# Two later layers' attention: maxima of the last two heads together, one bank for head outputs, another K tile order behind them

## The reference

```
for l in range(2):
    h = rmsnorm(x, norm_w[l])
    proj = h @ w_in[l]
    y_ssd = ssd_branch(...)          # 1024 features, ends in an rmsnorm over them
    y_cfm = conformer_branch(...)    # 512 features
    y_att = diff_attention_branch(...)  # 512 features, 4 heads of 128
    x = x + concat([y_ssd, y_cfm, y_att]) @ w_out[l]

diff_attention_branch, for each of 4 heads:
    s = q k^T / 8 for two halves c = 0, 1; causal mask; p = softmax(s)
    w = p[0] - lam * p[1];  o = w @ v
    o = rmsnorm(o, subln_w) * (1 - lambda_init);  result = o * silu(z)
```

## Time and profile before

| | us |
|---|---|
| median of three runs | 3719.62 (3715.02 to 3720.99) |
| the profiled execution | 3718.19 |
| its span in the trace | 3716.4 |
| TensorE busy | 3490.1, 94% of the span |
| VectorE busy | 1951.4, 53% |
| ScalarE busy | 545.5, 15% |

### The profile page before, as it was taken

The page is one execution under the profiler, slowest core; times in us unless marked ns, Lnnn a source line. Parts: engine busy times, 40 slices in busy tenths (PEclk is TensorE's granted clock), DMA queues, the critical chain, the costliest instruction groups (busy, mean ns, idle before and its releaser), DMA issues.

```text
span 3716.4 us, 54843 instructions
## 1 busy us (share of the span) xinstructions
PE 3490.1 (94%) x23714; PEld 2920.6 (79%) x23714; DVE 1951.4 (53%) x2736; ACT 545.5 (15%) x1020; POOL 161.1 (4%) x166
## 2 busy tenths in 40 slices
PE   6999999987889899998999999999899979999979
PEld 2445475545778889987999999998889958889958
DVE  2256942225667736533666667444375660375650
ACT  1000011223434321001100000000101120101120
POOL 0000001000000000000000000000040000140000
PEclk9999999998979999999999999999899989999979
DMA  8878633103322254443444444544344304344313
GB/s 344 329 308 323 260 110 114 57 3 92 81 70 70 59 202 170 170 170 125 159 165 169 163 169 169 183 180 159 109 152 149 136 35 147 114 152 155 125 38 133
DMA packets 134752, 559.44 MB, mean 151 GB/s; under 512 B 57504, under 2 KB 61856, under 8 KB 72112
## 3 DMA queue, kind: packets, MB, share of 16 engines
q1 hardware_dynamic: 120256, 456.17, 35.2%
q10 hardware_dynamic: 14304, 100.42, 6.8%
HBM read 539.24 MB, written 17.30 MB: 150 GB/s over the span
## 4 chain that ended last, share of the span: by engine, by line
PE 68%; DVE 4%; ACT 2%; issue 1%; SPq 1%; DMA 1%; DVEq 0%; ACTq 0%
PE ps L463 19%; PE ps L2576 13%; PE ps L2973 10%; PE ps L2632 7%; PE ps L2150 6%; PE ps L1590 2%; PE ps L3379 1%; PE ps L1688 1%; PE ps L1593 1%; DVE arena L2035 1%; DVE arena L2037 1%; SPq L1411 0%; PE ps L3085 0%; PE ps L3387 0%; PE ps L1569 0%
## 5 line engine op out<-in xcount | busy, mean ns | idle before, releaser
L463 PE MATMUL ps<-arena,ring 128*128 128x256 f32 (+3 forms) x4224 | 1073.3, 417 | 43.7 <-issue 20.2
L463 PEld LDWEIGHTS ps<-arena,ring 128*128 128x128 f32 (+1 forms) x4224 | 811.7, 193 | 304.2 <-issue 193.8
L2576 PE MATMUL ps<-arena 128*128 128x128 f32 x2560 | 292.4, 275 | 0.0
L2576 PEld LDWEIGHTS ps<-arena 128*128 128x128 f32 x2560 | 289.1, 192 | 0.0
L2576 PE MATMUL ps<-arena,ring 128*128 128x128 f32 x1920 | 220.9, 275 | 0.0
L2576 PEld LDWEIGHTS ps<-arena,ring 128*128 128x128 f32 x1920 | 217.7, 192 | 0.1
L2973 PE MATMUL ps<-arena 128*128 128x128 f32 x1792 | 204.7, 275 | 0.0
L2973 PEld LDWEIGHTS ps<-arena 128*128 128x128 f32 x1792 | 202.4, 192 | 0.0
L794 DVE SCALAR_TENSOR_TENSOR arena<-arena,small 128x512 f32<-128x512 f32 x240 | 180.4, 752 | 36.6 <-DMA arena<-in_ada_late 20.1
L2632 PE MATMUL ps<-arena 128*128 128x128 f32 x1408 | 161.2, 275 | 0.0
L2632 PEld LDWEIGHTS ps<-arena 128*128 128x128 f32 x1408 | 159.2, 192 | 0.0
(11 more groups left out here) (496 smaller groups left out, 4327.7 us busy)
## 6 DMA issues: line engine op xcount, KB each, us to landing
ring<-in_weights SPq DMA_DIRECT2D x402, 1024.0 KB, 4.8
arena<-in_ada_late ACTq DMA_DIRECT2D x64, 1024.0 KB, 8.0
arena<-in_gates SPq DMA_DIRECT2D x56, 256.0 KB, 3.7
arena<-in_front ACTq DMA_DIRECT2D x8, 1024.0 KB, 9.1
arena<-in_x ACTq DMA_DIRECT2D x2, 2048.0 KB, 12.5
keep_g<-arena SPq DMA_DIRECT2D x14, 256.0 KB, 2.0
arena<-keep_h SPq DMA_DIRECT2D x3, 1024.0 KB, 6.1
arena<-in_ctx ACTq DMA_DIRECT2D x1, 2048.0 KB, 23.6
```

The lines of the kernel that those rows point to most:

```text
L463: mm = M.matmul(o, ring[:, slot, k, c0:c0 + w], rhs, start=(kc == 0), stop=(kc == ktiles * WK - 1))
L2576: mm = M.matmul(o, w[:, k], x(k), start=(k == 0), stop=(k == HD - 1))
```

## The change

Three things are moved in both later layers; no arithmetic is added or taken away.
- The heads. PE's list has the same order. On ACT `turn(1)` now stands ahead of `exps(2)`, and `exps(3)` follows `exps(2)`. On DVE `outs(0)`, `outs(1)`, then `maxes` of heads 2 and 3, then `mix` of both, then the last two `outs`. All head outputs go through bank 7, so `values(h)` waits for `outs(h - 1)` from h = 1 on (before: from h = 2 on, for `outs(h - 2)`).
- The output product. `column_block` and `pairs` are replaced by `out_tiles`, which takes some K tiles of a block. The order is block 0 K tile 0, head norms, block 0 K tile 1, block 1 K tiles 0 and 1, block 0 K tiles 2 and 3, block 1 K tiles 2 and 3, then blocks 2 and 3 whole, without a loop. The wait for `om_in` stands ahead of block 1, the third wait for `y_part` ahead of block 0's K tile 2.
- The packed array has tiles 2 to 5 of `w_out_2` in the new order.

```diff
@@ packing
-        out += [...] + [_tiles(a['w_out_2'][l])]
+        out += [...] + [_tiles(a['w_out_2'][l])[OUT2_ORDER]]
+OUT2_ORDER = [0, 1, 4, 5, 2, 3, 6, 7, 8, 9, 10, 11, 12, 13, 14, 15]
@@ att_pe
-                if h >= 2:
+                if h >= 1:
                     p.wait_ge(at['o_in'].sem, at['o_in'].due(p))
-                o = ps[:, 6 + h % 2, 0:T]
+                o = ps[:, 7, 0:T]
...
+            def out_tiles(b, kts, first, last):
+                for kt in kts:
+                    slot = take_tile(p)
+                    for n in range(4):
+                        for k in range(WK):
+                            mm = M.matmul(ps[:, 4 * (b % 2) + n, 0:T], ring[:, slot, k, n * P:(n + 1) * P], yv[:, 4 * kt + k],
+                                          start=(kt == first and k == 0), stop=(kt == last and k == WK - 1))
+                            if n == 0 and k == 0:
+                                mm.then_inc(slot_left.sem, slot_left.up(p))
+                    if kt == last:
+                        mm.then_inc(bo.full[b % 2].sem, bo.full[b % 2].up(p))
...
-            column_block(p, bo, 0, 4, out_moving, before=(ssd_part, lambda: None, conformer_part, attention_part))
-            column_block(p, bo, 1, 4, out_moving)
-            pairs(p, 1, 4, out_moving, bo)
+            p.wait_ge(bo.free[0].sem, bo.free[0].due(p))
+            p.wait_ge(y_part.sem, y_part.due(p, 2))
+            out_tiles(0, (0,), 0, 3)
+            head_norms()
+            out_tiles(0, (1,), 0, 3)
+            p.wait_ge(bo.free[1].sem, bo.free[1].due(p))
+            p.wait_ge(at['om_in'].sem, at['om_in'].due(p))
+            out_tiles(1, (0, 1), 0, 3)
+            p.wait_ge(y_part.sem, y_part.due(p))
+            out_tiles(0, (2, 3), 0, 3)
+            out_tiles(1, (2, 3), 0, 3)
+            for b, kts in ((2, (0, 1, 2, 3)), (3, (0, 1, 2, 3))):
+                p.wait_ge(bo.free[b % 2].sem, bo.free[b % 2].due(p))
+                out_tiles(b, kts, 0, 3)
@@ att_act
-            for h in range(4):
-                turn(h)
-                if h < 2:
-                    exps(h + 2)
+            turn(0)
+            turn(1)
+            exps(2)
+            exps(3)
+            turn(2)
+            turn(3)
@@ att_dve
-                V.tensor_copy(oa[:, h], ps[:, 6 + h % 2, 0:T]).then_inc(at['o_in'].sem, at['o_in'].up(v))
+                V.tensor_copy(oa[:, h], ps[:, 7, 0:T]).then_inc(at['o_in'].sem, at['o_in'].up(v))
...
-            for h in range(4):
-                outs(h)
-                if h < 2:
-                    maxes(h + 2)
-                    mix(h + 2)
+            outs(0)
+            outs(1)
+            maxes(2)
+            maxes(3)
+            mix(2)
+            mix(3)
+            outs(2)
+            outs(3)
```

More of the change, by code:

```diff
@@ L95, in _pack_weights @@
         blocks = np.split(np.concatenate([ca, cg, bc, x, k, q, v, z, cz, az], 1), 12, 1)
-        out += [(_chunk_tiles if n in MIX_SEVEN else _tiles)(w) for n, w in enumerate(blocks)] + [_tiles(a['w_out_2'][l])]
+        out += [(_chunk_tiles if n in MIX_SEVEN else _tiles)(w) for n, w in enumerate(blocks)] + [_tiles(a['w_out_2'][l])[OUT2_ORDER]]
     return np.concatenate(out, 0)
@@ L2905, in build_program @@
         N = {n: again(f"b2_{n}") for n in (
-            "dt_mm z_in expd lnd dt_in a_in acs_mm acs_in v_mm v_in xs_mm xdt_in cb_mm cb_in "
+            "dt_mm z_in lnd dt_in a_in v_mm xs_mm cb_mm "
             "conv silu glu_s glu taps taps_pool ea "
-            "bc_mm diff dec dmul y_mm y_out out_mm out_in").split()}
+            "bc_mm diff dec dmul y_mm y_out").split()}
         def norm2_pe(p, l):
@@ L3398, in build_program, with ssd_act @@
         rms_s = rms(ys, 8, T, 1024, sqs, rs_s, bank=7)
-        def ssd_act(a):
+        def ssd_act(a, l):
             for h in range(S_HEADS):
@@ L3448, in build_program, with att_pe @@
         out_moving = lambda kc: yv[:, kc, :]
-        def att_pe(p):
+        def att_pe(p, l):
             def scores(h):
@@ L3477, in att_pe @@
             rms_s[0](p)
-            for h in range(4):
-                values(h)
-                if h < 2:
-                    scores(h + 2)
+            values(0)
+            scores(2)
+            values(1)
+            scores(3)
+            values(2)
+            values(3)
             p.wait_ge(at['s_max'].sem, at['s_max'].due(p, 2))
             def head_norms():
-                p.wait_ge(at['o_in'].sem, at['o_in'].due(p, 2))
+                p.wait_ge(at['o_in'].sem, at['o_in'].due(p))
                 p.wait_ge(at['osq'].sem, at['osq'].due(p))
@@ L3491, in head_norms, with att_act @@
                 mm.then_inc(at['om_mm'].sem, at['om_mm'].up(p))
[L3493 to L3502, removed]
-            column_block(p, bo, 0, 4, out_moving, before=(ssd_part, lambda: None, conformer_part, attention_part))
-            column_block(p, bo, 1, 4, out_moving)
-            pairs(p, 1, 4, out_moving, bo)
-        def att_act(a):
+            p.wait_ge(bo.free[0].sem, bo.free[0].due(p))
[12 more added lines that the diff above has]
+                out_tiles(b, kts, 0, 3)
+        def att_act(a, l):
             def exps(h):
@@ L3622, in out2_dve @@
                 h = b % 2
+                x = xT[:, 4 * b:4 * b + 4]
                 v.wait_ge(bo.full[h].sem, bo.full[h].due(v))
-                x = xT[:, 4 * b:4 * b + 4]
                 V.tensor_tensor(x, x, ps[:, 4 * h:4 * h + 4, 0:T], ALU.add).then_inc(nb["x_new"].sem, nb["x_new"].up(v))
@@ L3668, in _ @@
                 ssd_pe(pe)
-                att_pe(pe)
+                att_pe(pe, l)
         @block.scalar
@@ L3684, in _ @@
                 mix_act(act, l)
-                ssd_act(act)
-                att_act(act)
+                ssd_act(act, l)
+                att_act(act, l)
             store_act(act)
```

## The result

The changed kernel took 3695.01 us (median of six runs, 3686.07 to 3703.82) against 3718.19 us for the kernel before (six runs): ratio 0.9939, 95% interval 0.9922 to 0.9955, so 22.7 us less, between 17 and 29. The forecast was 3700.2 us in a range of 3695 to 3706. The median lies 5.2 us under the forecast, 0.01 us inside the range. The profiled execution took 3692.92 us.

What follows compares the result with a forecast made beforehand. TensorE, busy 94% of the span, was taken as the bound, so only its idle or low-clock time could be saved. From 3719.62 us, 9.72 + 5.22 + 4.48 = 19.42 us off gave 3700.2 us, range 3695 to 3706.

Steps and rivals of the forecast that it cites:

- the three places named: In both later layers: four attention heads (17.80 us), TensorE's 4.86 us idle in the output product, the 13 K tiles behind.
- Part 1, the wait: Output product: three K tiles cover the head norms' chain, so the 4.86 us wait goes in both layers, 9.72 us.
- the reserve: Output product: 20.75 us of tiles over an 11.77 us norm chain leave 8.98 us of slack.
- Part 2, the clock: K tiles behind the wait: without it TensorE's clock stays up, 5.22 us less over both layers; bounds 0 to 5.22.
- The first tiles: First two output tiles: slow clock cost left unchanged; bounds 3.33 us less to 1.89 us more.
- Part 3, the heads: Attention heads: new order hides both exponentials, 2.24 us less a layer, 4.48 in all; bounds 3.3 to -0.7 a layer.
- The stand for the shared bank: Heads: output 1's product waits for output 0's copy in bank 7, so DVE newly stands 1.84 us.
- The sum: Whole kernel: 9.72 + 5.22 + 4.48 = 19.42 us less, giving 3700.2 us, 0.52% less.
- A: Heads: the new stand and longer tail eat the hidden exponentials, so no gain there; 3704.7 us, chance 0.07.
- B: Output product: the clock falls or rises late in the first tiles, costing as much as before; 3705.4 us, chance 0.07.
- C: Output product: the weight stream becomes the bound; 3735 us at 8.0 us a tile; chance 0.02, shared with other losses.
- D: Output product: the wait moves to block 0's attention tile, so only the heads count; 3715.1 us, chance 0.02.

Runs made afterwards that it cites:

- e7: Changed kernel with the third y_part wait moved up one tile, leaving two tiles (13.83 us) of cover; 3696.91 us, ratio 0.9940.
- e5: Changed kernel with the third y_part wait moved up ahead of block 1's tile 0, leaving one tile of cover; 3712.57 us, ratio 0.9987.
- e4: Kernel before the change, with 11 never-read matmuls added where TensorE waits for the attention part; 3714.36 us, ratio 0.9986.
- e1: Changed kernel with the old output product put back, so only the head changes remain; 3711.75 us, ratio 0.9976.

## Why the prediction was right

**What bounds the kernel.** Right: all that the change gives is idle or slow time of TensorE at the three places named.

**Part 1, the wait.** Right in size: 9.72 us were put down and both waits are gone. The norms' chain took 11.67 us to VectorE's last step, as before (3065.75 - 3054.09 = 11.66; the 11.77 of the prediction runs on to TensorE's restart), and e7 shows that the reserve was there. e5 gives the wait back at 4.99 us a layer.

**Part 2, the clock.** Right: 5.22 us put down, 4.96 measured alone in e4, and the 15 tiles run at 0.2159 us a record. The first tiles were left as they were, with bounds of 3.33 less and 1.89 more. Over the full clock's price (6.92 us for one tile, 13.83 for two) they cost 3.33 us before, 0.64 + 0.65 in the first profile of the changed kernel and 1.69 + 1.62 in the second:

```profile
3035.76 8.61 PE ps L3480 x32
...
3578.63 8.54 PE ps L3480 x32
```

So this term is 2.0 us of gain in one execution and nothing in the other, of the same instructions. At half speed 1.05 us more for a tile is a rise that comes 2.1 us later. The Trainium skill (TensorE: Matmul & The Clock Gate, Part 1, "What's actually happening") lets the moment of the rise vary by half a microsecond either way. The two executions here lie 2.1 us apart, more than that allows, and the measurement decides. The prediction said that the 0.97 us between the layers of the kernel before agrees with that figure. This was misread: 0.97 us of cost is, by the same step, a rise that comes 1.9 us later. The bounds, 3.33 less and 1.89 more, were taken from rows and held.

**Part 3, the heads.** Right, a little small: 2.24 us a layer put down, 2.46 measured. The stand for the shared bank came out at 1.88 us for 1.84, both exponentials were hidden (they ended 0.4 and 0.2 us ahead of their mixes, for 0.2 and 0.07), and product 2 began 10.84 us behind the first copy for 10.79. The 0.22 us more is in the tail. Transposes 3 did follow product 2, but the steps cost less without a stand between them: from product 2's start to product 3's it took 2.86 us (3026.73 to 3029.59), not 1.65 + 1.47.

**The sum.** 19.42 us were put down. The changed code alone took 22.1 us less in the first profile and 20.1 in the second; the times say 22.7 (17 to 29) and 19.0 (14 to 24). What the first profile has over the sum are the first tiles' 2.0 us and the heads' 0.44. The stretches, 20.1 and 21.4 us shorter, come near these figures partly by chance: the first holds 2.5 us more ahead of the heads, the second 1.3 us less between the layers, neither from the change. The first median lies 5.2 us below the forecast. Of that, 1.4 us is the base (3719.62 in the forecast, 3718.19 in the six runs) and 2.5 us are the first tiles and the heads; the rest is less than what the part ahead of the change scatters by. That the median still fell inside the range, by 0.01 us, is luck; the mechanism and its terms are not.

**The rivals.** A (the heads give nothing) fell with e1, B (the clock does not come back) with the unbroken 103.61 us, C (the weight stream) with the same piece: 15 tiles without a stop (how much slack the stream had left, no run shows), D (the wait in a new place) with e5 and e7.

## What to carry to other kernels

A wait of TensorE costs more than it lasts: price the slow matmuls behind it from the trace, and find work that is ready to stand there; K tiles of another column block, whose operands are complete, cost nothing but an order of the weights. Two tiles were enough here, and a third bought nothing. When two heads' steps are interleaved so that one engine's wait lies under another's work, look which buffer is now shared (here one bank, 1.88 us a layer) and what fixed work (here the scaling) could go into the tail. To see 10 us in 3700, compare stretches of the trace and not only the medians, and take them around the changed code alone: here even unchanged matmuls ahead of it differed by 2.5 us with the clock.

## What the runs showed that I had not expected

The start of the later layers, ahead of which no kernel here differs, lay between 2592.6 and 2605.2 us in thirteen profiles: 12.6 us of scatter, over half of the effect. It is built up early: the first matmuls of the RWKV stage (L1443 before) start at 837.9 us in the profile of the kernel before, at 835.1 in the changed one, at 843.5 in e1. Its cause is open. Behind the mark two executions of the same kernel agreed within 1.3 us (1098.5 and 1097.2; 1087.8 and 1087.2), but the first pair did so by chance: in the second profile of the changed kernel the way to the first head copy was 2.5 us shorter and the way between the layers 0.9 us shorter, and the first tiles took 2.0 us more. From the mark to the end of the first SSD root's reciprocal (L505, L506) it was 416.6 to 417.3 us in seven of the thirteen profiles, 419.7 to 420.0 in the other six, and nothing between.
